# Two levels of a triangular inverse as 32x32 products, and fixed matmuls between the inverse and the state updates

## What is computed

```
A = where(strict, kk * dec * beta, 0)            # per head and chunk, C x C, strictly lower
sol = triangular_solve(I + A, [k * beta * exp(g), v * beta])
W, U0 = sol
for each chunk n:                                # the states, in order
    U = U0[n] - W[n] @ S
    O[n] = q_dec[n] @ S + qk[n] @ U
    S = g_last[n] * S + k_dec[n]^T @ U
```

## Time and profile before

| | |
|---|---|
| profiled execution, its own time | 1228.09 us |
| its span, first to last instruction | 1226.3 us |
| mean granted TensorE clock | 0.982 |
| PE busy | 1172.6 us (96%) |
| DVE busy | 853.8 us (70%) |
| ACT busy | 707.6 us (58%) |
| POOL busy | 59.4 us (5%) |
| chain that ended last, by engine | PE 87%, DVE 7%, ACT 4% |

### The profile page before, as it was taken

How to read it: one execution, slowest core, us unless ns; L and a number is a source line. 1 busy time by engine, 2 the same in 40 slices (tenths; PEclk the granted TensorE clock), 3 DMA queues, 4 the chain that set the end, 5 groups by cost and what they waited for, 6 DMA issues and landing times.

```text
span 1226.3 us, 27526 instructions
## 1 busy us (share of the span) xinstructions
PE 1172.6 (96%) x10101; PEld 1101.9 (90%) x10101; DVE 853.8 (70%) x1673; ACT 707.6 (58%) x1465; POOL 59.4 (5%) x66
## 2 busy tenths in 40 slices
PE   6999998999999999999999899999999999999997
PEld 5888887999999889998898799999988999899996
DVE  5888875777764477876435678774457887688874
ACT  7777755666554467764436466654546565555543
POOL 0000000111100000002000012110000000000000
PEclk9999999999999999999979999999999999999998
DMA  7343324355555444540101355656624443444431
GB/s 259 123 136 103 103 87 138 103 173 173 177 164 161 125 141 153 174 135 2 36 1 38 102 171 177 187 154 198 194 84 153 125 137 121 138 155 137 137 121 35
DMA packets 50087, 160.35 MB, mean 131 GB/s; under 512 B 5504, under 2 KB 8448, under 8 KB 49888
## 3 DMA queue, kind: packets, MB, share of 16 engines
q1 hardware_dynamic: 50016, 159.37, 41.6%
HBM read 158.30 MB, written 1.05 MB: 130 GB/s over the span
## 4 chain that ended last, share of the span: by engine, by line
PE 87%; DVE 7%; ACT 4%; issue 1%; DMA 0%; SPq 0%; ACTq 0%; DVEq 0%
PE banks L378 24%; PE banks L380 22%; PE banks L379 22%; PE banks L921 2%; PE banks L453 1%; ACT w_hi L359 1%; PE banks L901 1%; PE banks L886 1%; PE banks L500 1%; DVE m L533 1%; DVE w_lo L364 1%; PE banks L883 1%; PE banks L1567 1%; PE banks L1489 1%; PE banks L1558 1%
## 5 line engine op out<-in xcount | busy, mean ns | idle before, releaser
L364 DVE TENSOR_TENSOR w_lo<-raw,w_hi 128x1024 fp32r<-128x1024 f32 (+5 forms) x332 | 370.2, 1121 | 185.6 <-ACT w_hi L359 184.5
L378 PE MATMUL banks<-x_hi,w_hi 128*128 128x272 f32 (+2 forms) x1624 | 477.3, 294 | 7.0 <-DVE x_lo L513 3.6
L380 PE MATMUL banks<-x_hi,w_lo 128*128 128x272 f32 (+2 forms) x1624 | 464.5, 286 | 0.0
L379 PE MATMUL banks<-x_lo,w_hi 128*128 128x272 f32 (+2 forms) x1624 | 464.1, 286 | 0.0
L359 ACT ACTIVATE w_hi<-raw 128x1024 fp32r<-128x1024 f32 (+5 forms) x332 | 314.4, 955 | 99.3 <-PE banks L380 93.8
L378 PEld LDWEIGHTS banks<-x_hi,w_hi 128*128 128x128 f32 x1624 | 306.9, 189 | 19.6 <-issue 8.7
L379 PEld LDWEIGHTS banks<-x_lo,w_hi 128*128 128x128 f32 x1624 | 307.6, 189 | 0.1
L380 PEld LDWEIGHTS banks<-x_hi,w_lo 128*128 128x128 f32 x1624 | 307.3, 189 | 0.0
L378 PE MATMUL banks<-hid_hi,w_hi 128*128 128x272 f32 (+1 forms) x352 | 101.3, 288 | 0.0
L380 PE MATMUL banks<-hid_hi,w_lo 128*128 128x272 f32 (+1 forms) x352 | 99.8, 284 | 0.0
L379 PE MATMUL banks<-hid_lo,w_hi 128*128 128x272 f32 (+1 forms) x352 | 99.8, 284 | 0.0
(11 more groups left out here) (303 smaller groups left out, 1755.6 us busy)
## 6 DMA issues: line engine op xcount, KB each, us to landing
raw<-w_up SPq DMA_DIRECT2D x88, 512.0 KB, 4.4
raw<-w_attn SPq DMA_DIRECT2D x32, 512.0 KB, 4.4
raw<-w_dn SPq DMA_DIRECT2D x32, 512.0 KB, 4.2
raw<-w_moba SPq DMA_DIRECT2D x32, 512.0 KB, 3.9
raw<-w_down SPq DMA_DIRECT2D x32, 384.0 KB, 3.2
raw<-w_down SPq DMA_DIRECT2D x32, 320.0 KB, 3.2
raw<-w_mla SPq DMA_DIRECT2D x16, 384.0 KB, 3.5
raw<-w_attn_out SPq DMA_DIRECT2D x8, 512.0 KB, 3.9
```

Source lines behind the costliest of these rows:

```text
L364: nc.vector.tensor_tensor(w_lo[:, q, 0:wd], raw[:, q, 0:wd], w_hi[:, q, 0:wd].bitcast(F32), ALU.subtract).then_inc(lo_done, 1)
L378: nc.tensor.matmul(dst, hi, src[0][:, k, c0:c1], start=first, stop=False)
L379: nc.tensor.matmul(dst, hi, src[1][:, k, c0:c1], start=False, stop=False)
L380: return nc.tensor.matmul(dst, lo, src[0][:, k, c0:c1], start=False, stop=last)
```

## The change

Levels 1 and 2 compute only the three 32x32 diagonal blocks of each chunk, each from and to its own 32 rows. The banks 0 to 3, which DVE still reads over 96 rows, are written with zeros beforehand by four products of the identity with the cleared `x_st`. The fixed matmuls ahead of the levels go from 22 to 10. Eight fixed matmuls are added before the last two updates and seven behind them, ahead of the states, in bank 4. The semaphore `row_used` tells PE when DVE has read a row bank; the order of `ROW_BANK` follows.

```diff
-        ROW_BANK = (2, 7, 6, 1, 0, 5, 4)
+        ROW_BANK = (7, 6, 5, 4, 2, 1, 0)
...
-            keep_clock(22, 3)
+            keep_clock(10, 3)
+            pe.wait_ge(dn["clear"], 1)
+            for used, b in enumerate((3, 0, 1, 2)):
+                wait(pe, dn["row_used"], used)
+                nc.tensor.matmul(bank[b][0:C, 0:TP], ident[0:C, 0:C], x_st[:, 2, :], start=True, stop=True)
...
             def x_of(n):
...
-                        mm = nc.tensor.matmul(bank[n % 2][0:C, cc], a_tr[:, n % DNH, cc], d_in[:, n % DNH, cc], start=True, stop=True)
+                        for r, at in diagonal(c):
+                            mm = nc.tensor.matmul(bank[n % 2][r, at], a_tr[r, n % DNH, at], d_in[r, n % DNH, at], start=True, stop=True)
...
             def update(n):
...
-                        mm = nc.tensor.matmul(bank[2 + n % 2][0:C, cc], x_slot(n)[:, cc], d_tr[:, n % DNH, cc], start=True, stop=True)
+                        for r, at in diagonal(c):
+                            mm = nc.tensor.matmul(bank[2 + n % 2][r, at], x_slot(n)[r, at], d_tr[r, n % DNH, at], start=True, stop=True)
...
             for n in range(DNH, LEVELS * DNH + 4):
                 if n < LEVELS * DNH:
                     x_of(n)
+                if n >= LEVELS * DNH and n - 2 < LEVELS * DNH:
+                    pe.wait_ge(dn["d_in"], (LEVELS - 1) * DNH)
+                    keep_clock(4, 4)
                 if DNH <= n - 2 < LEVELS * DNH:
                     update(n - 2)
...
+            keep_clock(7, 4)
...
             for k in range(BASE - 1, 0, -1):
                 dve.wait_ge(dn["rows8"], BASE - k)
...
-                st(nc.vector.tensor_tensor(part3[:, :, 0:k], inv3[:, :, k:k + 1].to_broadcast([C, DNH * NC, k]), row, ALU.mult))
-                st.settle()
+                nc.vector.tensor_tensor(part3[:, :, 0:k], inv3[:, :, k:k + 1].to_broadcast([C, DNH * NC, k]), row,
+                                        ALU.mult).then_inc(dn["row_used"], 1)
+                dve.wait_ge(dn["row_used"], BASE - k)
...
+        def diagonal(c):
+            return [(slice(b, b + 32), slice(c * C + b, c * C + b + 32)) for b in range(0, C, 32)]
```

More of the change, by code:

```diff
@@ L342, in build @@
             "pair", "clear", "x", "x_out", "dd", "d", "t", "d_in", "ks", "r", "u", "u_out", "o", "o_out", "s_up", "s_new",
-            "osq", "osum", "oroot", "ohi", "olo", "oinv", "onorm", "ospread", "zero", "pads", "bgt_out", "eg", "ot", "block", "low", "v_last", "gates", "rows8", "unit", "from")}
+            "osq", "osum", "row_used", "oroot", "ohi", "olo", "oinv", "onorm", "ospread", "zero", "pads", "bgt_out", "eg", "ot", "block", "low", "v_last", "gates", "rows8", "unit", "from")}
         block = ctx.enter_context(nc.Block())
```

## The result

The changed kernel takes 1239.55 us (median of 4 runs, 1235.63 to 1246.37) against 1228.81 before, a ratio of 1.0093 with a 95% interval of 1.0070 to 1.0117: slower by 0.9%. Forecast were 1216.1 us and a range up to 1227. The last rival was priced at 1239.5 us. The profiled execution took 1241.63 us (span 1239.8), 13.5 more than the profiled execution before; the mean granted clock is 0.964 against 0.982.

The account below looks back on a forecast made before the run. PE was taken to bound the kernel, with half clock from 617.90 until 635. Savings of 5.1 (levels 1 and 2), 0.6 (last updates) and 7.4 (seam), less 1.1 added, took 1228.1 to 1216.1 us; range 1211 to 1227.

Parts of the forecast that it names:

- The last rival: Clock falls inside levels 1 and 2 because narrow products fill fewer cells, staying half to the states: 1239.5 us, chance 11%.
- Cost of a narrow product: Levels 1 and 2: 36 instructions at 10 ns take 0.37 us, making a turn 0.85 us against 1.27.
- The first rival: Levels 1 and 2: the three groups don't run together, 36 instructions cost 1.10 us; 1226.8 us, chance 12%.
- DVE's splits: Two turns in levels 1 and 2 have a DVE split of 1.14 us, each costing PE about 0.75.
- The last two updates of level 2: They fall into level 3's first turns and save 0.3 us each, 0.6 together.
- Ahead of the levels: Twelve fixed matmuls fewer, four zeroing products more, partly covered by PE's 0.90 us wait for DVE: costed at nothing.
- The seam: Before the states, 15 fixed matmuls add 1.1 us and hold the clock at full, saving 7.4 us in the states.
- the third rival: The same as the last rival: clock falls inside the levels, 1239.5 us, chance 11%.
- The 5.1 us forecast for levels 1 and 2: Saving from shorter narrow turns over 16 turns, values and splits included: 17.2 us in place of 22.34.

Follow-up runs that it names:

- few instructions: The changed kernel with levels 1 and 2 computed for the first chunk only, each 32x32 block against 96 moving columns, 6 instructions a product: 1218.55 us, ratio 0.9917.
- the seam alone: The kernel before, with only the 15 fixed matmuls added before the states (4, 4 and 7), levels 1 and 2 left whole: 1224.26 us, ratio 0.9965.
- the one with the hole of 1.91 us: The changed kernel with narrow products only in level 2 and the first four heads of level 1: 1241.95 us, ratio 1.0117.

## Why the prediction was wrong

*Cost of a narrow product.* Right: three groups run together at 12 ns an instruction (10 taken), 0.88 us a turn (0.85). With few instructions the two levels took 16.74 us (17.2). The first rival is out: the Trainium skill (TensorEngine Tiling (Array Packing), Gotcha 1: PSUM Pressure) says that row tiles can't use one bank at the same time, and here three tiles on separate rows write one bank with starts 12 ns apart. The measurement decides, for tiles that write separate partitions of the bank.

*DVE's splits.* The waits on them lasted 0.60 us each in the profile after and 0.65 with few instructions; 0.75 was taken. The last two updates of level 2 were to save 0.6: levels 3 and 4 took 18.43 us with few instructions and 19.05 with the seam alone.

*Ahead of the levels.* Costed at nothing, and right where the clock is whole: in all seven profiles of kernels with these edits where it is, the first transposes still wait 0.39 or 0.40 us for DVE, of 0.90 before. In the execution profiled after, the clock was at half there, and PE came last. Whether the change makes that likelier can't be told: five of twelve profiles with the 10 fixed matmuls had it, and one of four with the 22.

*The seam.* 7.4 saved and 1.1 added were forecast; alone it measured 7.2 and 1.4 in the profile, and 4.8 us between the medians of its own comparison.

*The step that failed* is the last sentence of the third rival, on which the sum rests: "The new turns are as full as level 3's unless DVE's splits open them." Every instruction was counted for its time on PE, none for its way to PE; the sum has no term for it. A turn went from 12 instructions of products to 36, each with a LDWEIGHTS of its own, and PE ran out of code at 0.9 us a turn, for 0.34 and, behind a transfer of weights, for 1.27 us. The clock fell behind the second hole. The 5.1 us forecast for levels 1 and 2 became 1.5. At half clock levels 3 and 4 took 11.8 us more than with the seam alone (30.89 against 19.05), and the 7.2 of the states were lost (36.15 against 29.00).

*The rival's price.* That 1239.5 stands so near 1239.55 is in part luck. The rival let the clock fall four turns into level 1 and put 6.2 us there, where it held until 598.0; it put 8 us into levels 3 and 4 and 2.9 into the fixed matmuls, where 13.3 were measured with both; and 2.1 us lie ahead of the levels, where it put nothing. Its reason was half right: it blamed the narrow products, which in three groups held the clock by themselves, and in one group, with a third of the work, did not.

*The sum.* Without holes on issue the forecast of 1216.1 stands beside 1218.55 measured, in a kernel that leaves out two of three chunks in these levels. Of the kernels that compute everything the lowest median was 1222.55.

What stays open: how much code per us PE can be given, and why its packets start some 58 instructions ahead; no run measures either by itself. That a code packet waits for a running weight load is read from the times of the packets; no run moves one against the other alone. Nor does any run vary the length of a single hole among narrow products.

## What to carry to other kernels

When a change multiplies the instructions of an engine for the same time, look at the place where it does and ask what brings the code; in the profile it shows as idle time put down to issue, at fixed places in the program and not in time. Look also at what the DMA carries just then: here the longest holes stood where a packet of code started only at the end of a weight load. Where TensorE's work is thin, price a hole by what the clock costs for as long as thin work follows, not by its own length: here 1.5 us cost 18. And try half of such a change: with narrow products in one level the clock held, and the kernel beat the one before and the changed one, though not the seam alone by more than the runs can tell.

## What the runs showed that was not expected

- With one hole of 1.85 us among whole 96x96 products the kernel took 22 us more (1246.68 against 1224.26), with one of 1.04 nothing that can be told (1224.86).
- Three 32x32 tiles on separate rows and columns write one PSUM bank with starts 12 ns apart.
- PE busy 30.90 of 30.90 us with narrow work did not raise the clock from half; nor did the first 16.86 of 16.90 us of the states.
- With 32x32 products in only one group at a time the clock fell 3.1 us into level 1, with PE busy 2.85 of 3.00 us and no hole on issue.
- In nine of the sixteen profiles a packet of code starts within 0.01 us of a weight load's last packet: 595.48 behind 595.47 in the profile after, 597.33 behind 597.32 in the one with the hole of 1.91 us.
